# Expert weights by rank: no expert loaded twice, five buffers, and a last norm on token rows

## The chip, the cores and the metric

One core of a Trainium2 chip runs the whole program. The metric is the device time in microseconds (us) of one execution, the median of several.

## What is computed

One inference step of a two-layer backbone over 384 tokens of width 1024: 128 prompt tokens and 256 sample tokens, all float32. Each layer has a mixer (layer 0: mLSTM and MLA attention; layer 1: SSD and gated DeltaNet) and then a mixture of 32 SwiGLU experts, of which each token uses two. At the end comes an RMS norm over each token's 1024 channels. The change touches the experts and the last norm, so this is the part of the reference that matters:

```python
def rms_norm(x, g):
    y = xf * lax.rsqrt(jnp.mean(xf * xf, axis=-1, keepdims=True) + EPS)
    return (y * g.astype(jnp.float32)).astype(x.dtype)

def hier_moe(h, P, l):          # top-1 group of 4, then top-2 of its 8 experts
    glog = (x @ P['moe_w_group'][l] + P['moe_b_group'][l]).astype(f32)
    gsel = jnp.argmax(glog, axis=-1)
    elog = jnp.take_along_axis(elog, gsel[:, None, None], axis=1)[:, 0]
    tv, ti = lax.top_k(elog, MOE_TOPK)
    tw = jax.nn.softmax(tv, axis=-1) * gw
    eid = gsel[:, None] * MOE_PER_GROUP + ti
    hg = jnp.einsum('nd,edf->nef', x, P['moe_w_gate'][l])     # 1024 -> 256
    hu = jnp.einsum('nd,edf->nef', x, P['moe_w_up'][l])
    act = jax.nn.silu(hg) * hu * combine[..., None].astype(x.dtype)
    y = jnp.einsum('nef,efd->nd', act, P['moe_w_down'][l])    # 256 -> 1024

y_prompt = rms_norm(x, norm_final)      # and the same for y_sample
```

One expert's three matrices are 1 MiB each, 3 MiB together.

## The kernel before, in words

Five engines run their own instruction lists and wait for each other by semaphores. x, h and the mixer's output lie transposed in SBUF (channels on the 128 partitions, 8 blocks of 384 tokens): `xT`, `hT`, `mix`. Jobs of TensorE take the eight PSUM banks in rotation, in an order written out in `plan_jobs` (L160).

**Routing.** After the output projection (L870, L1100) TensorE turns the amplified rows back to tokens (`rows_out`, L1147) and ScalarE copies them, scaled, into `hrows`, which lies in `mix`; GpSimd adds the shift (L736) and SP writes them to memory (`h_rows_out`, L579). Meanwhile VectorE works out the router (L1991 to L2105): the two experts of each token, each token's rank inside its expert (by matmuls, `ranks`, L1123), and from these a slot. Expert e has 64 slots (`CAP`). One unit of work is a pair of blocks of 64 slots: pair q holds experts q and 16 + q. A 17th pair holds two spare blocks: an expert with 65 to 128 tokens gets one of them for those beyond 64, and is then loaded a second time (L2055 to L2064 choose, L2092 to L2101 give its number and the flag). If a third expert has more than 64, or one more than 128, the flag is set and all experts are computed densely instead (`dense`). `slot_lists` (L1137) turns the slots by matmuls into token numbers per slot (`slot_token`, L2086).

**A pair.** GpSimd gathers the pair's 128 rows by an indirect DMA (L745), TensorE transposes them (`turn`, L1170), ScalarE copies them to SBUF (L1607). Gate-up (L1183) is 32 matmuls of 512 columns, two at a time on the two halves of the array, one half for each block; silu (L1615) and the product (L2113) follow, a transposition (L1194), a copy (L2117), and the down product (L1208). ScalarE and VectorE scale the two halves of the rows (L1623, L2122), and GpSimd scatters them into `y_rows` in memory (L756). The turn of the next pair goes between gate-up and the transposition. After the last scatter SP reads the rows of each token's two experts back (L657), VectorE adds them (L2176), TensorE transposes them (L1264), and VectorE adds them to xT (L1984).

**Weights.** SP issues them (`load_pair`, L588): two buffers of a pair, one in the arena, one in the ring that the projections' weights use otherwise, so four experts in all. The first pair's go out before the output projection, the second's after it. The gate and up matrices of pair n (n from 2) wait for the gate-up of pair n - 2, its down matrices for the down product of pair n - 2. The order of the pairs is `ORDER`: the spare pair comes ninth, its two expert numbers are read from SBUF into SP's registers.

**The last norm.** ScalarE squares xT block by block (L1454), TensorE adds over the channels with a matrix of ones (L913), ScalarE takes the root (L1456), VectorE the reciprocal (L1781) and scales eight blocks by it and by the gain (L1788), TensorE turns them to token rows (L1426), ScalarE copies them to `mix` (L1742), and GpSimd issues the three output DMAs (L821).

## Time and profile before

| what | value |
|---|---|
| median of three runs (lowest, highest) | 1618.92 us (1618.03, 1621.61) |
| the profiled execution's own time | 1612.7 us |
| its span, first to last instruction | 1610.9 us |
| busy: TensorE, VectorE, ScalarE, GpSimd | 1317.4, 530.8, 343.9, 129.4 us |
| mean granted TensorE clock | 0.886 of full speed |
| moved by DMA | 341.77 MB, mean 212 GB/s |

A page line of a group has the form: line, engine, operation, output<-inputs and shapes, xcount, then busy us, mean ns of one, and the idle time of the engine ahead of it with what ended most of it. Line numbers are those of the kernel before. Times of the timeline and the chain are us from the span's start. A row "issue" is time for which the profile shows no releaser; SPq is SP's DMA issue.

### The profile page before, as it was taken

Reading aid. Unit: us, or ns where it says so; the run is one execution under the profiler, and the core shown is the slowest. Engines: PE = TensorE matmul, PEld = TensorE weight load, DVE = VectorE, ACT = ScalarE, POOL = GpSimd, SP = SyncE. Lnnn points to the kernel's source line nnn. Section 1 sums busy time; section 2 is a strip of 40 time slices with the busy share of each in tenths; the row PEclk is TensorE's granted clock in tenths of the full one; section 3 lists DMA queues with packets and bytes.
Section 4 is the critical chain, followed back from the end, with each engine's and each line's share of the span. In section 5 each row is a group of like instructions: output and inputs, shape, how many; then the busy total and the mean of one; then the engine's idle time right before and its main releaser. Section 6 shows DMA issues by size and latency. Waiting matters only on the chain.

```text
span 1610.9 us, 16071 instructions
## 1 busy us (share of the span) xinstructions
PE 1317.4 (82%) x6198; PEld 804.4 (50%) x6198; DVE 530.8 (33%) x1067; ACT 343.9 (21%) x720; POOL 129.4 (8%) x145
## 2 busy tenths in 40 slices
PE   5999799877986888878499997888859788888763
PEld 3545584344783333323266547787859633333322
DVE  3010652322233110101456907677651511010113
ACT  2100313322221111111326213222231211111102
POOL 2400100000011111110000001000000111111100
PEclk8999888877897999989799999999878789999986
DMA  9943565165534999997514100000034569999951
GB/s 340 322 152 106 189 192 209 55 224 191 184 124 180 420 423 422 420 413 290 204 57 153 66 13 1 27 1 1 1 105 183 196 255 422 423 421 419 405 206 72
DMA packets 82881, 341.77 MB, mean 212 GB/s; under 512 B 18967, under 2 KB 20161, under 8 KB 56560
## 3 DMA queue, kind: packets, MB, share of 16 engines
q1 hardware_dynamic: 67952, 313.09, 49.3%
q0 software_dynamic: 14848, 27.58, 5.3%
q8 instruction: 53, 0.87, 0.2%
q14 instruction: 28, 0.23, 0.0%
HBM read 333.11 MB, written 30.58 MB: 226 GB/s over the span
## 4 chain that ended last, share of the span: by engine, by line
PE 70%; DVE 14%; issue 9%; DMA 2%; ACT 2%; SPq 0%; POOL 0%; DVEq 0%; ACTq 0%; POOLq 0%
PE psum L870 19%; PE psum L1183 17%; PE psum L962 8%; PE psum L1208 8%; PE psum L894 3%; PE psum L1170 2%; PE psum L957 2%; DVE arena L2231 1%; DVE mix L2191 1%; PE psum L1083 1%; PE psum L1063 1%; PE psum L901 1%; DMA arena<-y_rows 1%; PE psum L913 1%; PE psum L1194 1%
## 5 line engine op out<-in xcount | busy, mean ns | idle before, releaser
L1183 PE MATMUL psum<-arena 128*64 128x512 f32 x576 | 153.1, 692 | 45.9 <-issue 43.6
L870 PE MATMUL psum<-hT,ring 128*128 128x384 f32 x448 | 152.4, 504 | 7.0 <-ACT hT L1463 5.1
L1183 PE MATMUL psum<-ring,arena 128*64 128x512 f32 x512 | 119.8, 622 | 19.4 <-issue 19.4
L962 PE MATMUL psum<-ring 128*128 128x128 f32 x872 | 114.8, 290 | 17.7 <-issue 8.4
L1183 PEld LDWEIGHTS psum<-arena 128*64 128x64 f32 x576 | 51.4, 158 | 146.4 <-issue 143.2
L2113 DVE TENSOR_TENSOR arena<-arena,psum 128x256 f32<-128x256 f32 x34 | 14.3, 421 | 332.9 <-ACT arena L1615 332.9
L870 PEld LDWEIGHTS psum<-hT,ring 128*128 128x128 f32 x448 | 88.3, 198 | 69.7 <-issue 12.8
L962 PEld LDWEIGHTS psum<-ring 128*128 128x128 f32 x872 | 109.1, 203 | 22.9 <-issue 13.1
L870 PE MATMUL psum<-ring,hT 128*128 128x512 f32 (+2 forms) x336 | 116.1, 507 | 0.0
L870 PE MATMUL psum<-mix,ring 128*128 128x384 f32 x256 | 91.7, 515 | 0.0
L1615 ACT ACTIVATE arena<-psum 128x256 f32<-128x256 f32 x34 | 13.1, 384 | 365.1 <-PE psum L1183 365.1
L1183 PEld LDWEIGHTS psum<-ring,arena 128*64 128x64 f32 x512 | 42.9, 143 | 95.6 <-issue 95.6
L870 PEld LDWEIGHTS psum<-ring,hT 128*128 128x128 f32 x336 | 58.3, 190 | 57.2 <-issue 56.4
L870 PEld LDWEIGHTS psum<-mix,ring 128*128 128x128 f32 x256 | 79.5, 316 | 5.8 <-issue 3.8
L1208 PE MATMUL psum<-arena 128*64 128x512 f32 x288 | 65.8, 598 | 9.3 <-DVE arena L2117 9.3
L756 POOL DMA_INDIRECT y_rows<-arena,slot_row x34 | 34.1, 1003 | 459.9 <-DVE arena L2122 430.3
L2122 DVE TENSOR_SCALAR arena<-psum,share 128x512 f32<-128x512 f32 x34 | 25.5, 751 | 127.8 <-PE psum L1208 127.8
L1208 PE MATMUL psum<-ring,arena 128*64 128x512 f32 x256 | 58.5, 599 | 8.3 <-DVE arena L2117 8.3
L894 PE MATMUL psum<-ring,sil 128*32 128x512 f32 x384 | 58.7, 762 | 6.2 <-issue 6.2
L736 POOL TENSOR_TENSOR mix<-mix,arena 128x1024 f32<-128x1024 f32 x6 | 14.1, 2369 | 509.1 <-ACT mix L1597 509.1
L1984 DVE SCALAR_TENSOR_TENSOR xT<-psum,modT,xT 128x128 f32<-128x128 f32 x64 | 23.8, 413 | 82.2 <-PE psum L870 79.6
L2231 DVE SCALAR_TENSOR_TENSOR arena<-arena,colsT 128x388 f32<-128x388 f32 x80 | 49.8, 623 | 2.8
(474 smaller groups left out, 1654.0 us busy)
## 6 DMA issues: line engine op xcount, KB each, us to landing
ring<-in_ada_w SPq DMA_DIRECT2D x24, 2048.0 KB, 10.6
arena<-in_moe_w_gate SPq DMA_DIRECT2D x36, 1024.0 KB, 11.9
arena<-in_moe_w_up SPq DMA_DIRECT2D x36, 1024.0 KB, 14.4
arena<-in_moe_w_down SPq DMA_DIRECT2D x36, 1024.0 KB, 17.5
ring<-in_moe_w_gate SPq DMA_DIRECT2D x32, 1024.0 KB, 14.1
ring<-in_moe_w_up SPq DMA_DIRECT2D x32, 1024.0 KB, 16.6
ring<-in_moe_w_down SPq DMA_DIRECT2D x32, 1024.0 KB, 18.2
ring<-in_w_in_odd SPq DMA_DIRECT2D x7, 2048.0 KB, 7.9
```

The costliest lines, as they stand in the source:

```text
L756: pool.indirect_dma_start(out=y_dram[l], out_offset=bass.IndirectOffsetOnAxis(ap=slot_row[:, q:q + 1].bitcast(U32), axis=0), in_=yrow[u], ...
L870: ins = mm(out, lhs(k), rhs(k), start=(k == 0), stop=(k == n - 1))
L894: ins = mm(b[at_:at_ + 32, :], sil[:, 4 * half + k, :], w[half][:, k, parity::2], start=(k == 0), stop=(k == 3), tile_position=(0, at_))
L901: ins = mm(b[:, 4 * m:4 * m + 4], mod_rows[:, m::4], pick, start=True, stop=True)
L957: ins = mm(b[:, tok(h)], col(h).to_broadcast([P, P]), ident, start=True, stop=True)
L962: ins = mm(b[:, h * width:(h + 1) * width], lhs(h), rhs(h), start=True, stop=True)
L1170: ins = nc.tensor.transpose(psum[:, k // 4, tok(k % 4)], hrow[q % 2][:, tok(k)], ident)
L1183: ins = mm(psum[half, 2 + s, :].rearrange("p (w f) -> p w f", w=2), hg[s][:, k, half], pair_gu[s][h][:, :, k, :], start=(k == 0), stop=(k ...
L1208: ins = mm(psum[half, 5 + n, :], act_s[s][:, j, half], pair_dn[s][h][:, j, 512 * n:512 * n + 512], start=(j == 0), stop=(j == 1), tile_pos ...
L1984: ins = stt(xT[:, m, t0:t1], bank(name, l, m)[:, t0:t1], modT[:, l, part, m, j:j + 1], xT[:, m, t0:t1], ALU.mult, ALU.add)
L2122: ts(yrow[q % 2][:, 512:D], psum[:, 6, :], share[:, ORDER[q]:ORDER[q] + 1], None, ALU.mult).then_inc(S(f"{kind}yb"), 1)
L2231: ins = stt(conv[:, i, :], cin[:, i, w:w + COUT], wcol[w], conv[:, i, :], ALU.mult, ALU.add)
```

## The change

**Units instead of pairs.** There are still 17 units. The first two hold experts 0 and 16, 1 and 17, as before. The next two are each a whole unit of 128 slots for one expert: the two experts with the most tokens (of all but 0, 16, 1, 17, 15, 31). The other units hold two experts of 64 slots. The places that the two fullest leave empty are filled by experts 15 and 31, whose own places were given up. So every expert is loaded once, 32 loads instead of 34, and from unit 2 on SP reads each expert's number from SBUF (`expert_id`, new) into a register. The flag is set if any expert has more tokens than slots.

**Five buffers.** Place n (one expert) goes to buffer n mod 5: two in the arena, two in the ring, and a new one over `hT` and `mix`, which now lie side by side as `wide`. Its load waits for the expert numbers and for the token rows' write to memory. Each place's gate and up matrices wait for the gate-up of the unit that used the buffer five places earlier, and its down matrix for that unit's down product; a unit's two gate-up loads stand ahead of its two down loads in SP's queue. The dense path computes its h anew from xT.

**The last norm** works on token rows: TensorE turns xT half by half (four blocks each) as soon as the residual adds allow, ScalarE squares the rows out of PSUM with a running sum, takes a root per tile, and VectorE scales out of PSUM into `mix` by the token's factor and the gain row, which GpSimd loads ahead of the second expert layer.

```diff
-SPARE = 2
-BLOCKS = EXPERTS + SPARE
-PAIRS = BLOCKS // 2
 HALF = EXPERTS // 2
-ORDER = list(range(HALF // 2)) + [PAIRS - 1] + list(range(HALF // 2, HALF))
-SPARE_AT = ORDER.index(PAIRS - 1)
+DOUBLES = 2
+AHEAD = 2
+BUFFERS = 5
+UNITS = [(2 * n, 2 * n + 1) for n in range(AHEAD)] + [(2 * AHEAD + n,) * 2 for n in range(DOUBLES)]
+UNITS += [(n, n + 1) for n in range(2 * AHEAD + DOUBLES, EXPERTS, 2)]
+PAIRS = len(UNITS)
+UNIT_OF = [next(u for u, two in enumerate(UNITS) if n in two) for n in range(EXPERTS)]
+MOVED = (HALF - 1, EXPERTS - 1)
+SINGLE = [h * HALF + n for n in range(AHEAD) for h in range(2)] + list(MOVED)
...
-    jobs += norm(4) + [("fin", c, k // 4) for c in range(TILES) for k in range(0, KD, 4)]
+    jobs += [("fin", c, half) for half in range(2) for c in range(TILES)]
...
+        def landed(l, n):
+
+            k = n % BUFFERS
+            return (EXPERTS + BUFFERS - 1 - k) // BUFFERS * l + n // BUFFERS + 1
...
-        hT = sb("hT", [P, KD, T])
-        mix = sb("mix", [P, KD, T])
+        wide = sb("wide", [P, 2 * KD * T])
+        hT = wide[:, 0:KD * T].rearrange("p (k t) -> p k t", k=KD)
+        mix = wide[:, KD * T:2 * KD * T].rearrange("p (k t) -> p k t", k=KD)
...
+        def expert_buffer(words):
+            return (words[:, 0:gate_up_words].rearrange("p (w k f) -> p w k f", w=2, k=KD),
+                    words[:, gate_up_words:gate_up_words + down_words].rearrange("p (j d) -> p j d", j=2))
+
+        one = gate_up_words + down_words
+        buffers = [(gu[n], dn[n]) for n in range(2)] + [expert_buffer(ring_words[:, n * one:(n + 1) * one]) for n in range(2)]
+        buffers += [expert_buffer(wide[:])]
...
-            def load_pair(l, n):
...
+            def load_unit(l, u):
+
+                kind = "gathered_"
+                weights_ = expert_weights(l)
+                which = sorted(set(UNITS[u]))
+                ids = []
+                for n in which:
+                    if u < AHEAD:
+                        ids.append(HALF * (n % 2) + u)
+                        continue
+                    at = n - 2 * AHEAD if u < AHEAD + DOUBLES else DOUBLES + HALF * (n % 2) + u - DOUBLES
+                    ids.append(sp.value_load(expert_id[0:1, l, at:at + 1], min_val=0, max_val=EXPERTS - 1))
+                for n, e in zip(which, ids):
+                    if n >= BUFFERS:
+                        sp.wait_ge(S(f"{kind}gu_computed"), PAIRS * l + UNIT_OF[n - BUFFERS] + 1)
+                    for w in range(2):
+                        sp.dma_start(buffers[n % BUFFERS][0][:, w],
+                                     weights_[w][bass.ds(e, 1)].rearrange("e (p k) f -> p (e k) f", k=KD))\
+                          .then_inc(S(f"{kind}gu{n % BUFFERS}_in"), 16)
+                for n, e in zip(which, ids):
+                    if n >= BUFFERS:
+                        sp.wait_ge(S(f"{kind}y1_computed"), PAIRS * l + UNIT_OF[n - BUFFERS] + 1)
+                    sp.dma_start(buffers[n % BUFFERS][1], weights_[2][bass.ds(e, 1)].rearrange("e (p j) d -> p (e j) d", j=2))\
+                      .then_inc(S(f"{kind}dn{n % BUFFERS}_in"), 16)
...
-                load_pair(l, 0)
+                load_unit(l, 0)
                 sp.wait_ge(*computed("o", l, KD - 1))
-                load_pair(l, 1)
+                load_unit(l, 1)
                 h_rows_out(l)
-                for n in range(2, PAIRS):
-                    load_pair(l, n)
+                sp.wait_ge(S("expert_ids"), l + 1)
+                sp.wait_ge(S("h_rows_out"), 16 * TILES * (l + 1))
+                for u in range(AHEAD, PAIRS):
+                    load_unit(l, u)
...
+                pool.wait_ge(S("odd_rows"), 2)
+                pool.dma_start(gain_row[:, 0:D], along(a["norm_final"])).then_inc(S("final_gain_in"), 16)
...
-                    pe.wait_ge(S(f"{kind}gu{s}_in"), 64 * loads(l, q))
+                    for n in sorted(set(UNITS[q])):
+                        pe.wait_ge(S(f"{kind}gu{n % BUFFERS}_in"), 32 * landed(l, n))
...
-            pe.wait_ge(S("h_final"), KD)
-            for c in range(TILES):
-                for half in range(2):
+            for half in range(2):
+                pe.wait_ge(*x_ready(4, 4 * half + 3))
+                for c in range(TILES):
                     b = issue("fin", c, half)
                     for k in range(4):
-                        ins = nc.tensor.transpose(b[:, tok(k)], hT[:, 4 * half + k, tok(c)], ident)
+                        ins = nc.tensor.transpose(b[:, tok(k)], xT[:, 4 * half + k, tok(c)], ident)
...
+            fn(rs_col[:, TILES:TILES + 1], eps[:, 0:1], ACT.Sqrt)
+            for half in range(2):
+                for c in range(TILES):
                     act.wait_ge(*computed("fin", c, half))
-                    dst = mix[:].rearrange("p k t -> p (k t)")[:, c * D:(c + 1) * D]\
-                        .rearrange("p (q k) -> p k q", k=KD)[:, 4 * half:4 * half + 4, :]
-                    fn(dst, heads(bank("fin", c, half), 4), ACT.Copy).then_inc(S("y_rows"), 1)
+                    done(fn(final_squares, bank("fin", c, half), ACT.Square,
+                            accum_out=row_sums[:, half, c:c + 1]), "final_sums")
+                    if half:
+                        fn(rs_col[:, c:c + 1], row_sums[:, 1, c:c + 1], ACT.Sqrt, scale=1.0 / D,
+                           bias=row_sums[:, 2, c:c + 1]).then_inc(S("final_roots"), 1)
+                if half == 0:
+                    done(fn(row_sums[:, 2, :], row_sums[:, 0, :], ACT.Identity, scale=1.0 / D, bias=eps[:, 0:1]), "final_sums")
...
-                o_(tt(prod, both, base_slot.unsqueeze(1).unsqueeze(1).to_broadcast(all4), ALU.mult))
-                o_(v.tensor_reduce(base_, prod, AX, ALU.add))
...
+                o_(stt(key, counts, 64.0, place, ALU.mult, ALU.add))
+                o_(v.tensor_reduce(top, key, AX, ALU.max))
+                o_(ts(doubled[:, 0, :], key, top, None, ALU.is_equal))
+                o_(stt(key2, doubled[:, 0, :], -1e7, key, ALU.mult, ALU.add))
+                o_(v.tensor_reduce(second, key2, AX, ALU.max))
+                o_(ts(doubled[:, 1, :], key2, second, None, ALU.is_equal))
+                o_(tt(shifts, doubled[:], delta, ALU.mult))
+                tt(room_, doubled[:, 0, :], doubled[:, 1, :], ALU.add)
+                tt(at_home, home, shifts[:, 0, :], ALU.add)
+                o_(v.tensor_reduce(hole_sum, shifts, AX, ALU.add))
+                ts(room_, room_, float(CAP), CAP + 0.5, ALU.mult, ALU.add)
+                o_(tt(at_home, at_home, shifts[:, 1, :], ALU.add))
+                o_(tt(at_home[:, HALF - 1::HALF], hole, hole_sum, ALU.subtract))
                 dve.wait_ge(*computed("rk", l))
                 order = bank("rk", l)[:, 0:TILES * EXPERTS].rearrange("p (c e) -> p c e", c=TILES)
                 where = R[11][:, :, 0:EXPERTS]
-                o_(stt(where, order, CAP + 0.5, bc(move, 1, [P, TILES, EXPERTS]), ALU.is_gt, ALU.mult))
-                take(tt(where, where, order, ALU.add), "rk", l)
+                tt(over, order, bc(room_, 1, [P, TILES, EXPERTS]), ALU.is_gt)
+                take(tt(where, order, bc(at_home, 1, [P, TILES, EXPERTS]), ALU.add), "rk", l)
+                o_(stt(where, over, float(OOB), where, ALU.mult, ALU.add))
                 o_(tt(prod, both, bc(where, 1, all4), ALU.mult))
                 o_(v.tensor_reduce(slot, prod, AX, ALU.add))
-                o_(tt(slot, slot, base_, ALU.add))
...
+                ids = R[3][0:1, 0, 0:DOUBLES + EXPERTS]
+                o_(tt(shifts[0:1], doubled[0:1], fill[0:1], ALU.mult))
+                tt(ids[:, DOUBLES:], iota[0:1, 0:EXPERTS], shifts[0:1, 0, :], ALU.add)
+                o_(v.tensor_reduce(fill_sum[0:1], shifts[0:1], AX, ALU.add))
+                tt(ids[:, 0:DOUBLES], vacant[0:1], fill_sum[0:1], ALU.subtract)
+                o_(tt(ids[:, DOUBLES:], ids[:, DOUBLES:], shifts[0:1, 1, :], ALU.add))
+                done(ts(expert_id[0:1, l, :], ids, 1.0, None, ALU.mult), "expert_ids")
...
+                take(tt(key, counts, room_, ALU.is_gt), "ct", l)
+                o_(v.tensor_reduce(too_many, key, AX, ALU.max))
+                done(ts(flag[0:1, l:l + 1], too_many[0:1], 0.5, None, ALU.is_gt), "flag")
...
+            dve.wait_ge(S("final_gain_in"), 16)
+            for c in range(TILES):
+                dve.wait_ge(S("final_roots"), c + 1)
+                o_(v.reciprocal(rs_col[:, c:c + 1], rs_col[:, c:c + 1]))
+                for half in range(2):
+                    part = slice(4 * half, 4 * half + 4)
+                    dst = mix[:].rearrange("p k t -> p (k t)")[:, c * D:(c + 1) * D]\
+                        .rearrange("p (q k) -> p k q", k=KD)[:, part, :]
+                    stt(dst, heads(bank("fin", c, half), 4), rs_col[:, c:c + 1], final_gain[:, part, :],
+                        ALU.mult, ALU.mult).then_inc(S("y_rows"), 1)
```

## Rows read from the trace of the kernel before

**Rows 1.** Page, part 2 (40 slices) and one line group of part 5.

```profile
DMA  9943565165534999997514100000034569999951
GB/s 340 322 152 106 189 192 209 55 224 191 184 124 180 420 423 422 420 413 290 204 57 153 66 13 1 27 1 1 1 105 183 196 255 422 423 421 419 405 206 72
...
L870 PE MATMUL psum<-hT,ring 128*128 128x384 f32 x448 | 152.4, 504 | 7.0 <-ACT hT L1463 5.1
```

**Rows 2.** Busy us by engine (x instructions), granted clock, DMA share and GB/s, two windows.

```profile
520.00:540.00 20.00, 19.18 (x96) 7.43 (x92) 2.29 (x5) 3.17 (x5) 4.05 (x4) 1.00 1.02 421
620.00:640.00 20.00, 16.01 (x66) 5.67 (x62) 1.60 (x3) 2.59 (x4) 2.01 (x2) 0.83 1.01 421
```

**Rows 3.** SP's weight issues in the first expert layer: start, us, first of each kind.

```profile
512.90 0.33 SPq L601 DMA_DIRECT2D arena<-in_moe_w_gate  x1
...
525.81 0.33 SPq L601 DMA_DIRECT2D ring<-in_moe_w_gate  x1
...
538.29 0.33 SPq L601 DMA_DIRECT2D arena<-in_moe_w_gate  x1
...
589.06 0.80 SPq L606 DMA_DIRECT2D ring<-in_moe_w_down  x2
601.46 0.37 SPq L601 DMA_DIRECT2D arena<-in_moe_w_gate  x1
```

**Rows 4.** TensorE's waits in the first and the second expert layer: us, times, longest.

```profile
PE psum L1183 <- issue: 30.1, 13, 4.0
...
PE psum L1183 <- issue: 32.9, 12, 4.7
```

**Rows 5.** The chain in the first expert layer, start and us.

```profile
543.87 6.87 PE psum L1183 x32
...
556.35 3.99 issue
560.34 9.82 PE psum L1183 x32
...
754.10 7.10 PE psum L1183 x32
```

**Rows 6.** First gather's issue; then gathers and scatters of two windows, us to landing.

```profile
497.18 1.08 POOL L745 DMA_INDIRECT arena<-h_rows,slot_token  x1 [12.72 <-DVE slot_token L2086]
...
arena<-h_rows,slot_token POOLq DMA_INDIRECT x1, 3.3
...
y_rows<-arena,slot_row POOLq DMA_INDIRECT x1, 8.2
arena<-h_rows,slot_token POOLq DMA_INDIRECT x1, 10.0
```

**Rows 7.** VectorE in the slot arithmetic: first and eleventh instruction, and after the lists.

```profile
487.28 0.19 DVE L2055 SCALAR_TENSOR_TENSOR crowded<-psum,cst 128x32 f32<-128x32 f32 x1
...
489.73 0.26 DVE L2068 SCALAR_TENSOR_TENSOR route<-psum,route 128x96 f32<-128x96 f32 x1 [0.20 <-PE psum L1133]
...
496.16 0.18 DVE L2086 TENSOR_SCALAR slot_token<-psum 128x17 int32<-128x17 f32 x1 [1.98 <-PE psum L1143]
```

**Rows 8.** The end of the kernel (timeline), and VectorE's row scaling (groups of instructions).

```profile
1577.32 6.19 DVE L1984 SCALAR_TENSOR_TENSOR xT<-psum,modT,xT 128x128 f32<-128x128 f32 x16 [1.07 <-PE psum L1264]
...
1585.96 0.58 ACT L1456 ACTIVATE rB<-psum,eps 128x384 f32<-128x384 f32 x1 [0.59 <-PE psum L913]
1586.64 2.55 DVE L1781 RECIPROCAL rB<-rB 128x384 f32<-128x384 f32 x1 [3.13 <-ACT rB L1456]
1589.23 4.32 DVE L1788 SCALAR_TENSOR_TENSOR hT<-xT,gains,rB 128x384 f32<-128x384 f32 x8
...
1593.61 4.33 PE L1426 MATMUL psum<-cst,hT 128*128 128x128 f32 x24 [7.69 <-DVE hT L1788]
1594.82 5.73 ACT L1742 ACTIVATE mix<-psum 128x512 f32<-128x512 f32 x6 [8.28 <-PE psum L1426]
...
L2122 DVE TENSOR_SCALAR arena<-psum,share 128x512 f32<-128x512 f32 x17 | 12.8, 751 | 63.9 <-PE psum L1208 63.9
```

125 lines of the change are left out of this document (45 added, 80 removed).

## The prediction

> **What bounds the kernel now.** I began with the page's slices [rows 1]. In two stretches, slices 13 to 18 and 33 to 37, the DMA digits stand at 9 and the rate at 405 to 423 GB/s; these are the expert layers. Elsewhere the rate is mostly below 260. Next came the busy times of two windows inside the first expert layer [rows 2]: the DMA share is 1.01 to 1.02 in both, at 421 GB/s, but TensorE is 96% busy in the first and 80% in the second, where its granted clock is 0.83, a mean between the two levels of 1.2 and 2.4 GHz. So the stage changes its bound. The chain shows where [rows 5]: the gate-up of a pair takes 6.87 us without a wait before it up to 543.87; the next one stands still for 3.99 us and then takes 9.82 us. TensorE's waits in each expert layer are put down to "issue" [rows 4], 13 times 30.1 us and 12 times 32.9 us. No engine released them, and only the weights' semaphores are left at that place, so these are landings. From the fifth pair on the weight stream is the bound, and TensorE is the bound for the first four pairs.
>
> Two prices follow. An unhindered pair costs TensorE what lies between the SP issues of two pairs, which wait for gate-ups: 525.81 - 512.90 = 12.9 us, then 538.29 - 525.81 = 12.5 us [rows 3]. A streamed pair costs more: gate-up 4 starts at 560.34, gate-up 16 at 754.10 [rows 5], 193.8 / 12 = 16.15 us, or 8.1 us per expert (3 MiB, with the gathers and scatters that run beside it). The stream itself starts at 512.90 [rows 3] and traffic some 1.6 us later. Up to gate-up 16 it carries 15 pairs less the last two down matrices, 29.33 experts: (753 - 514.5) / 29.33 = 8.13 us each. The two agree, so the stream never ran dry before, and a load that isn't made is worth its full 8.13 us as long as the stream stays the bound at the end.
>
> **The change, part by part, for one layer.** The sum is over the start of the last unit's gate-up; what comes behind it is the same.
>
> 1. Loads. 34 expert loads become 32. Units 0 and 1 are loaded early as before. Behind the restart there are then 28 experts instead of 30: 2 x 8.13 = 16.3 us less.
>
> 2. The fifth buffer. Expert place 4 goes into hT and mix, which are free once the token rows have been written to memory. Its load needs no gate-up of unit 0 any more, only the register value and that write. The expert numbers are worked out in the idle 1.98 us in which VectorE waits for the slot lists, ahead of the conversion at 496.16 [rows 7]; six instructions of at most 0.19 us fit there. So this load runs in a stretch in which the stream stands still, from about 498 to 506: another 8.1 us off the stream.
>
> 3. What is given back. TensorE now needs fewer experts for its first units (unit u needs 2u of them, where pair u needed 2u + 2), so it runs at 12.5 us per unit for longer, and the stream runs ahead until no buffer is free. By hand: the gate-up matrices of place 11 wait for unit 4's gate-up, which ends at 512.9 + 4 x 12.5 = 562.9, traffic from 564.5. The stream has by then carried places 5 to 10 without the last down matrix, 5.67 x 8.13 = 46.1 us, and is dry at 560.6: 3.9 us lost. From unit 9 on the stream is the bound again: TensorE could start it at 512.9 + 8 x 12.5 + 5.7 = 618.6, the stream has brought place 17's gate-up at 514.5 + 3.9 + 12.33 x 8.13 = 618.6.
>
> So far: last gate-up at 514.5 + 26.33 x 8.13 + 3.9 = 732.5 instead of 753, 20.5 us less.
>
> 4. The start is later. In the slot arithmetic the ten instructions from 487.28 to 489.73, 0.20 of it a wait for the ranks [rows 7], become thirteen, each (2.45 - 0.20) / 10 = 0.225 us, so 0.65 to 0.7 us more; two on the ranks become three; L2072 goes, and two more that ran under a wait. That is 0.7 + 0.3 - 0.2 less the wait of 0.20 that they now fill, 0.6, say 0.5 us. All of it is ahead of the first gather, hence of the first gate-up.
>
> 5. The first gather beside expert 4's load. Alone a gather lands in 3.3 us; it is issued at 497.18 [rows 6] and gate-up 0 hangs on it. Beside a full stream a scatter takes 8.2 us, and 10.0 for a gather queued behind one [rows 6]. So the new neighbour costs between 0 and 4.9 us. I take 2.8, because here the stream only begins as the gather does. The gathers of units 1 and 2 have the whole of gate-up 0 to land in.
>
> Steps 4 and 5 shift the restart of the stream 1:1: 3.3 us. A layer gains 20.5 - 3.3 = 17.2, with ends 20.5 and 20.5 - 0.5 - 6.7 (10.0 - 3.3) = 13.3. Two layers: 34.4, ends 26.6 and 41.
>
> A rule on step 5 is in the Trainium skill, "DMA: Bandwidth & Descriptors", section "Queues, rings and completion order": an engine alternates between the rings it has work for, a packet from each in turn, and so a gather does not queue behind all of expert 4's load. By it the wait grows with the gather's own packets only; if each waits for one like it, about 3.3 us more, and the two layers would give 33.4. The scatter's 8.2 beside a stream with no gap leans the same way as the rule, and neither excludes the other.
>
> 6. Costed at nothing. The new waits on SP (register values, rows written): queued behind them are all later loads, but the old queue stood there until 512.90 anyway. Reading the registers: the queue had two of these reads between the down issue at 589.06 and 601.46 [rows 3], where it waited for a gate-up in any case; the stream has more than a pair's work outstanding then, which is the cover. The gain row for the last norm (512 KB on POOL's queue) goes out before the expert layer, when the stream is idle. The flag is ready some us later, long before anyone asks for it. Matmuls per unit don't change in number or shape.
>
> **The last norm.** Residual adds end at 1577.32 + 6.19 = 1583.5 [rows 8]. Now come the sum over channels, the root 1585.96, a 384-wide reciprocal of 2.55, eight scalings of 4.32, transposes, and six copies that end at 1594.82 + 5.73 = 1600.55 [rows 8]. After: the transposes of half 0 go beside the residual adds, and so do their three squares. Behind the last add: four transposes (4/24 x 4.33 = 0.7, plus a 0.3 handover), one square with its sum on ScalarE (about 1.0, as one copy's 5.73/6), root and one-column reciprocal 0.5, then six scalings on VectorE. A 512-wide pass over PSUM takes 0.751 there [rows 8]; the new one writes with a stride, as the ScalarE copy did at 0.955. Six at 0.8 with two more reciprocals: 5.2. End 1583.5 + 1.0 + 0.2 + 1.0 + 0.5 + 5.2 = 1591.4, so 9.1 us less; with 1.13 per scaling 7. I take 9.
>
> **Sum.** 34.4 + 9 = 43.4 us off the profiled execution's 1612.7: 1569.3. That execution stands 6.2 us below the median of the three runs, 1618.92; the forecast is for the median, 1618.92 - 43.4 = 1575.5, written 1576.
>
> **The rivals.**
> A. Gather undisturbed. If the first gather lands before expert 4's descriptors matter, step 5 costs nothing: 1618.9 - 2 x 20 - 9 = 1570. For it: the first gather brings 21 rows in the first layer and 71 in the second, by the reference's choices. Against: they start within a microsecond of each other.
> B. Register reads hold up SP. No row times one by itself; the bound from above is half of 601.46 - 589.86, 5.8 us. Two now stand ahead of each unit's loads, between a down and the next gate-up load. As long as one takes under 2 us the outstanding work covers it; at 5.8 the stream would run dry early in each unit as long as TensorE sets the pace, and a layer loses a further 7 us: 1590. The Trainium skill, same page, "Latency and other measured facts", gives about 600 ns as the floor of such a read, by which this rival falls away.
> C. The early part brings nothing. The fifth buffer's 8.1 us is eaten by more starvation, as four buffers' worth of order is left and TensorE's pace is not kept (gate-ups of 9.82 instead of 6.87 in the first nine units too, as after the wait in rows 5). Then only the bytes count: 2 x (16.3 - 3.3) + 8 = 34 less, 1585.
> D. Slower: an expert that can't be doubled. The places of experts 0, 1, 15, 16, 17 and 31 are fixed, so one of these with over 64 tokens, which before got a spare block, now raises the flag, and all 32 experts are computed densely. A gate-up there would be 32 matmuls of 384 columns at 504 ns [rows 1], 16 us, so over 500 us a layer. It decides from one such expert on. Against it: counting the reference's choices on its inputs, over 64 are expert 28 in the first layer (71) and 22 and 23 in the second (67 and 70), none of the six.
> E. The change doesn't do what it says: if the double unit waited for a second landing the kernel would hang rather than be slow, so only a stream that isn't the bound is left. Rows 2 speak against it: then 1618.9 - 9 = 1610.
>
> **How the numbers follow.** Forecast's own case 0.5 (1567 to 1584), A 0.17, B 0.1, C 0.13, D 0.02, E 0.05, the rest is unnamed. The range 1562 to 1594 takes in A, B and C with the spread of the runs (3.6 us) at either end. About 0.2%, 3.2 us, is what can be told from no change. Faster by more 0.94, within 0.02, slower 0.04 (D and what I don't see).
>
> **What would show it.** In the profile after: places 4's load issued about 497, ahead of the first gate-up; turn 0 at 502 to 506 instead of 500.63; gate-ups 12.5 us apart up to unit 8 or 9, then waits of 2 to 4 us; TensorE's "issue" waits near 20 us per layer instead of 30; weights 12.6 MB fewer; last ScalarE copies gone, three roots in their place, end some 8 us behind the last residual add. Wrong would be: gate-ups 16 us apart from unit 4 on, a DMA rate that falls under 400 for more than 5 us after 520, or a first gate-up later than 512.

## The result, and the profile after

The changed kernel takes 1591.82 us, the median of four runs (1590.08 to 1592.47); beside it the kernel before took 1620.26 (four runs, 1618.03 to 1624.00). The ratio is 0.9828, with a 95% interval from 0.9808 to 0.9849. So 28.4 us went, where 43.4 were forecast. The direction is right and the time lies in the range, near its upper end; a third of the forecast gain is missing, and the runs below are about that third.

The page of the changed kernel, parts 2 and 5, beside [rows 1]:

```profile
PEclk9999888777695999899799999989787969999996
DMA  9942565055517799998514200000017259999943
GB/s 343 333 150 106 188 199 212 0 212 212 187 52 286 287 391 418 418 419 353 202 54 150 75 14 0 4 25 1 1 41 264 119 201 407 398 418 418 417 195 122
...
L1204 PE MATMUL psum<-cst,arena 128*128 128x128 f32 x272 | 38.8, 288 | 18.9 <-DMA arena<-h_rows,slot_token 18.9
```

The first expert layer shows 9 in four slices of the DMA line instead of five, the second in five as before, and their middle runs at 417 to 419 GB/s instead of 419 to 423. The last row is new: turn 0 waited 18.9 us in the two layers for the first gathers.

The timeline of the changed kernel from the first gather to the second unit (start, us, engine, line; in brackets the idle time before and what ended it), beside [rows 3, 6]:

```profile
504.78 0.37 SPq L630 DMA_DIRECT2D wide<-in_moe_w_gate  x1
...
505.72 0.38 SPq L636 DMA_DIRECT2D wide<-in_moe_w_down  x1
527.55 0.35 SPq L630 DMA_DIRECT2D arena<-in_moe_w_gate  x1
...
532.65 0.33 SPq L636 DMA_DIRECT2D arena<-in_moe_w_down  x1
534.31 0.33 SPq L630 DMA_DIRECT2D arena<-in_moe_w_gate  x1
...
505.88 1.09 POOL L777 DMA_INDIRECT arena<-h_rows,slot_token  x1 [12.85 <-DVE slot_token L2130]
...
514.19 1.94 PE L1204 MATMUL psum<-cst,arena 128*128 128x128 f32 x8 [9.42 <-DMA arena<-h_rows,slot_token]
517.30 9.62 PE L1218 MATMUL psum<-arena 128*64 128x512 f32 x32 [1.17 <-ACT arena L1642]
```

Place 4's load goes out 1.1 us ahead of the gather. The gather lands 8.2 us after its issue, where it took 3.3 alone. From 532.65 to 534.31 SP issues a down load, reads two registers and goes on: 1.33 us behind the issue, 0.67 for a read and what goes with it.

The chain of the same layer, beside [rows 5], and TensorE's waits from 500 to 770, beside [rows 4]:

```profile
595.02 6.89 PE psum L1218 x32
602.07 0.33 SPq L630
602.50 18.23 DMA arena<-in_moe_w_up
620.98 7.10 PE psum L1218 x32
...
726.76 24.16 DMA arena<-in_moe_w_up
750.93 0.28 issue
751.20 7.10 PE psum L1218 x32
```

```profile
PE psum L1204 <- DMA arena<-h_rows,slot_token: 9.4, 1, 9.4
PE psum L1218 <- DMA arena<-in_moe_w_up: 8.8, 4, 3.9
...
PE psum L1218 <- DMA ring<-in_moe_w_up: 6.3, 3, 3.9
PE psum L1218 <- DMA wide<-in_moe_w_up: 5.4, 2, 3.5
```

Gate-ups are 12.5 us apart up to unit 7; unit 8's, at 620.98, is the first to wait, and from there a unit takes 16.3 us ((751.20 - 620.98) / 8). The waits for weights add to 8.8 + 6.3 + 5.4 = 20.5 us, where "issue" stood with 30.1; in the second layer they add to 24.1, where it stood with 32.9.

The end (timeline), beside [rows 8]:

```profile
1565.03 6.19 DVE L2018 SCALAR_TENSOR_TENSOR xT<-psum,modT,xT 128x128 f32<-128x128 f32 x16 [1.08 <-PE psum L1300]
...
1572.02 0.60 ACT L1775 ACTIVATE arena<-psum 128x512 f32<-128x512 f32 x1 [0.71 <-PE psum L1461]
...
1573.37 2.17 DVE L2424 SCALAR_TENSOR_TENSOR wide<-psum,rs_col,gain_row 128x512 f32<-128x512 f32 x2
...
1577.90 2.17 DVE L2424 SCALAR_TENSOR_TENSOR wide<-psum,rs_col,gain_row 128x512 f32<-128x512 f32 x2
```

The last scaling ends at 1580.07, 8.85 us behind the last residual add (1571.22); before, the last copy ended 17.04 us behind it.

**One layer measured in two parts.** The document goes on with three landmarks. T0 and T16 are the ends of the first and the last gate-up (the start of ScalarE's activation behind them). Between them lies the fall-off, the first of two slices of 1 us in a row in which the DMA engines move under 380 GB/s, at the end of the layer's stream. "Full" is from T0 to the fall-off, "tail" from there to T16. The tail ends with the last gate-up itself, so the table also has that gate-up's own time and the stretch from T0 to its start, which is what the forecast was over: 20.5 us shorter. Where the text says stream, it means T0 to T16. Per layer, mean of both layers, in us:

```
kernel                       full    tail   T0 to T16   last gate-up   T0 to its start   first gather (layer 0, 1)
before, two profiles        235.4    13.5     248.8         7.5            241.3         3.3, 3.9 / 3.3, 3.7
after, two profiles         215.5    17.4     232.9         8.2            224.7         8.2, 8.3 / 8.1, 8.4
held gather                 215.3    18.9     234.3         9.4            224.8         3.3, 4.0
place 4 loaded late         220.8    19.5     240.3         8.5            231.8         3.4, 4.1
before, spare not loaded    225.2    12.3     237.5         7.1            230.4         3.4, 4.0
second double at 14         212.7    18.7     231.4         7.9            223.4         3.4, 4.1
doubles at 8 and 14         212.3    19.8     232.1         7.1            225.0         3.3, 4.3
held gather, no scatters    213.4     9.9     223.3         8.0            215.3         3.4, 4.1
rows spread                 216.5    14.0     230.4         7.9            222.6         3.1, 3.9
rows in stride 8            214.4    19.7     234.1         7.1            227.0         3.2, 4.3
rows spread, double at 14   213.3    14.7     228.0         7.1            220.8         3.0, 3.8
```

The full part became 20.0 us shorter, the tail 3.9 us longer, and the last gate-up starts 16.6 us earlier. The boundary between full and tail is good to a slice, about 1 us. Single layers differ: the tail was 13.2, 11.8, 13.8 and 15.0 us before and 15.3, 18.8, 15.6 and 20.0 after. Part of that is TensorE's clock in the last gate-up, which took between 7.1 and 10.1 us. First the kernel after (the gate-up at 751.20), then the kernel with the held gather (744.27), whose TensorE had waited 3.17 us ahead of it:

```profile
751.20:758.30 7.10, 7.09 (x32) 2.62 (x32) 0.36 (x1) 0.00 (x0) 0.99 (x1) 1.00 0.14 53
```

```profile
744.20:754.30 10.10, 10.01 (x32) 3.13 (x32) 0.00 (x0) 0.00 (x0) 0.00 (x0) 0.70 0.10 38
```

The granted clock was 1.00 in the one and 0.70, a mean between the two levels, in the other.

**The same stretch in bytes.** From T0 to the start of the last gate-up the DMA engines moved 99.3 MB before and 90.2 MB after: 9.1 MB less, 21.7 us at 420 GB/s. Against that rate they lost 4.8 us before and 9.9 after, 5.1 more: 2.5 in the idle stretch of step 3, 1.5 in the first 25 us behind T0, 0.8 behind the fall-off, the rest spread. 21.7 - 5.1 = 16.6. By the fall-off alone they had moved 10.1 MB less, so 1.0 MB more is left for the tail, 2.4 us of its length.

The fall-off in slices of 1 us; the first row is of the kernel before, from 730 to 770, the second of the kernel after, from 710 to 750:

```profile
GB/s 442 426 418 401 410 410 442 426 426 418 442 397 463 402 410 426 410 442 328 270 229 197 188 188 123 115 217 57 20 4 0 0 0 0 0 0 0 0 8 66
```

```profile
GB/s 410 410 426 426 418 426 418 410 426 434 410 418 426 377 442 406 410 418 414 418 418 426 426 410 426 410 426 426 410 430 430 418 385 360 328 311 279 303 262 205
```

### The profile page after: what moved, and what is told of

It reads as the page before. It is cut to its first block, busy times and chain, and to the rows that moved or that the text cites. A ratio compares the mean times of both kernels' runs of the same rounds, so it can differ in the third digit from the quotient of the medians.

```text
span 1590.6 us, 16451 instructions
## 1 busy us (share of the span) xinstructions
PE 1306.8 (82%) x6182; PEld 798.6 (50%) x6182; DVE 528.8 (33%) x1064; ACT 338.9 (21%) x722; POOL 130.4 (8%) x146
## 4 chain that ended last, share of the span: by engine, by line
PE 59%; DMA 18%; DVE 13%; issue 6%; ACT 2%; SPq 1%; POOL 0%; DVEq 0%; ACTq 0%; POOLq 0%
PE psum L904 20%; PE psum L1218 11%; PE psum L996 9%; DMA ring<-in_moe_w_up 6%; DMA arena<-in_moe_w_up 5%; PE psum L1244 3%; PE psum L928 3%; DMA wide<-in_moe_w_up 3%; PE psum L991 2%; DVE arena L2269 1%; DVE wide L2229 1%; PE psum L1097 1%; PE psum L1117 1%; PE psum L935 1%; DMA arena<-h_rows,slot_token 1%
## 5 line engine op out<-in xcount | busy, mean ns | idle before, releaser
L904 PE MATMUL psum<-wide,ring 128*128 128x384 f32 x704 | 242.9, 506 | 7.0 <-ACT wide L1498 5.1
L904 PEld LDWEIGHTS psum<-wide,ring 128*128 128x128 f32 x704 | 167.4, 240 | 74.7 <-issue 15.4
L1218 PE MATMUL psum<-arena 128*64 128x512 f32 x480 | 160.6, 667 | 24.5 <-DMA ring<-in_moe_w_up 11.8
L1218 PE MATMUL psum<-ring,arena 128*64 128x512 f32 x384 | 133.1, 611 | 12.1 <-DMA wide<-in_moe_w_up 10.8
L904 PE MATMUL psum<-ring,wide 128*128 128x512 f32 (+2 forms) x336 | 116.1, 507 | 0.0
L1218 PE MATMUL psum<-wide,arena 128*64 128x512 f32 x224 | 90.8, 623 | 10.3 <-DMA arena<-in_moe_w_up 10.3
L904 PEld LDWEIGHTS psum<-ring,wide 128*128 128x128 f32 x336 | 58.3, 190 | 57.2 <-issue 56.4
L1244 PE MATMUL psum<-arena 128*64 128x512 f32 x240 | 73.0, 598 | 8.3 <-DVE arena L2153 8.3
L1244 PE MATMUL psum<-ring,arena 128*64 128x512 f32 x192 | 65.7, 598 | 6.2 <-DVE arena L2153 6.2
L1204 PE MATMUL psum<-cst,arena 128*128 128x128 f32 x272 | 38.8, 288 | 18.9 <-DMA arena<-h_rows,slot_token 18.9
L1204 PEld LDWEIGHTS psum<-cst,arena 128*128 128x128 f32 x272 | 30.5, 145 | 45.2 <-issue 45.2
## 6 DMA issues: line engine op xcount, KB each, us to landing
arena<-in_moe_w_up SPq DMA_DIRECT2D x28, 1024.0 KB, 22.6
ring<-in_moe_w_up SPq DMA_DIRECT2D x24, 1024.0 KB, 18.9
```

What stands on the lines that cost most here:

```text
L904: ins = mm(out, lhs(k), rhs(k), start=(k == 0), stop=(k == n - 1))
L1204: ins = nc.tensor.transpose(psum[:, k // 4, tok(k % 4)], hrow[q % 2][:, tok(k)], ident)
L1218: ins = mm(psum[half, 2 + s, :].rearrange("p (w f) -> p w f", w=2), hg[s][:, k, half], buffers[UNITS[q][h] % BUFFERS][0][:, :, k, :], star ...
L1244: ins = mm(psum[half, 5 + n, :], act_s[s][:, j, half], buffers[UNITS[q][h] % BUFFERS][1][:, j, 512 * n:512 * n + 512], start=(j == 0), sto ...
```

## The experiments

Twelve runs, on three chips, each set beside runs of the kernel before on the same chip: 1619.73 in the first set, 1620.73 in the second, 1619.62 in the third.

**1. The kernel after, a second time.** No edit.

> The changed kernel itself, as the standard for the others of this set, and a second profile of it. Theory clock: the 8 us by which the first expert layer began later in the profile of after than in that of before (weights of unit 1 issued at 478.6 instead of 470.0) lie in code that the change did not touch and come from where the granted clock fell in the attention stage, so this start moves by several us from one profile to the next; here anywhere from 466 to 482. Rival layout: the change did it (other SBUF addresses, a larger table), then 478 to 479 again. Time 28 us below before.

1586.97 us (1585.56 to 1592.27), ratio 0.9797 (0.9776 to 0.9818), so 32.8 us less. The second profile gives streams of 231.6 and 235.2 us, the first 231.4 and 233.4, and the first gathers agree to 0.1 us. But layer 0 begins elsewhere: unit 1's weights are issued at 475.3, against 478.3 in the first profile and 470.0 in that of the kernel before. That speaks against the rival, which wanted 478 to 479 again.

**2. The last norm alone.** The kernel before with the norm on token rows, experts untouched:

```
+            for half in range(2):
+                pe.wait_ge(*x_ready(4, 4 * half + 3))
+                for c in range(TILES):
+                    b = issue("fin", c, half)
                     for k in range(4):
-                        ins = nc.tensor.transpose(b[:, tok(k)], hT[:, 4 * half + k, tok(c)], ident)
+                        ins = nc.tensor.transpose(b[:, tok(k)], xT[:, 4 * half + k, tok(c)], ident)
...
```

> Only the last norm is changed, the experts are those of before. By the rows of the two profiles the stretch from the start of the last residual adds to the last write of the output rows went from 23.2 to 15.0 us, so 8.2 us below before, ratio 0.995. If the adds themselves or the output transfers took the gain back, the ratio is over 0.997. Rival layout for the start of the first expert layer: it is at 470 as in before; theory clock: anywhere from 462 to 482.

1612.07 us (1602.29 to 1616.15), ratio 0.9942 (0.9918 to 0.9966): 7.7 us. In its trace the last scaling again ends 8.9 us behind the last add. The norm is worth about 8 us (5.5 to 13.3 by the interval). Its experts are those of before, and yet unit 1's weights go out at 475.3, as in the second profile of the kernel after.

**3. The gather held free of the load.** In the kernel after, SP waits for the first gather before it issues place 4's load:

```
                 for u in range(AHEAD, PAIRS):
+                    if u == AHEAD:
+                        sp.wait_ge(S("gathered_hrow0_in"), 16 * loads(l, 0))
                     load_unit(l, u)
```

> After, but SP waits with the load of place 4 until the first gather has landed. Theory: the first gather took 8.2 and 8.3 us instead of 3.3 and 4 because this load runs beside it; held back, the gather lands in 3.3 to 4 us, the load still ends before the first gate-up does, and each layer ends 4.5 us earlier: 9 us below after. Rival: the gather is slow for another reason (its place in the queue, the memory it reads), then it takes 8 us again and the later load costs nothing or a little: 0 to 4 us above after.

1580.61 us (1570.89 to 1585.96), ratio 0.9750 (0.9720 to 0.9779), 6.4 us faster than the kernel after on the same chip, where 9 were expected; the two intervals just touch. From its chain:

```profile
504.48 3.27 DMA arena<-h_rows,slot_token
...
507.88 1.96 PE psum L1205 x8
```

The gather is back at 3.3 and 4.0 us. So the neighbour had cost 4.9 and 4.4 us, about the 4.9 that step 5 named as the most it could cost. The load, now issued at 508.80, still lands just before the stream restarts (519.82, T0 519.94), and the last gate-up starts as far behind T0 as in the kernel after, 224.8 against 224.7 us. The 1.4 us per layer that the stream is longer are the last gate-up's: it took 9.4 us on average instead of 8.2, by the clock. By its median this kernel beats both.

**4. Place 4 loaded late.** The fifth buffer is there, but its load waits for unit 0's gate-up:

```
                 for u in range(AHEAD, PAIRS):
+                    if u == AHEAD:
+                        sp.wait_ge(S("gathered_gu_computed"), PAIRS * l + 1)
                     load_unit(l, u)
```

> After, but the load of place 4 waits for the first gate-up, as the first load behind the restart did in before: the fifth buffer's head start is gone, the saved loads stay. Theory (the prediction's terms, corrected to what after shows): 4.6 us per layer back from the gather, 7.5 us of weights added to the stream, 2 us less starvation, so 1 us per layer above after, 0 to 4 us in all. If the head start is worth its full 8.1 us per layer: 7 us above after. If it was worth nothing: 9 us below after, as hold_gather.

1591.15 us (1587.66 to 1596.87), ratio 0.9823 (0.9798 to 0.9849), 10.5 us slower than the held gather and 4.2 slower than the kernel after, whose interval it overlaps. The last gate-up starts 231.8 us behind T0, against 224.8 held and 224.7 after: loading place 4 ahead is worth 7.0 us a layer, the idle stretch that comes with it already taken off. This kernel doesn't have that stretch. In the kernel after it is where step 3 put it, from 572 on, 46 us behind T0 (rate in slices of 1 us, from 560 to 600):

```profile
GB/s 418 434 410 430 402 430 414 434 422 402 410 410 393 352 287 307 180 160 176 438 430 418 410 442 434 418 410 369 397 422 418 430 401 438 418 418 401 418 451 434
```

The seven slices from 393 to 176 miss 2.6 us of full rate, and the same stretch of the second layer 1.7; 3.9 were forecast.

**5. The price of a load.** The kernel before, without the spare pair's loads; the two spare experts are computed with what lies in the buffers:

```
             def load_pair(l, n):
...
+                if n == SPARE_AT:
+                    return
...
-                    pe.wait_ge(S(f"{kind}gu{s}_in"), 64 * loads(l, q))
+                    if q != SPARE_AT:
+                        pe.wait_ge(S(f"{kind}gu{s}_in"), 64 * weights_in(l, q))
```

> The kernel before, without the weight loads of the spare pair (12.6 MB fewer in the two layers); TensorE does not wait for them and multiplies what lies in the buffers, so the two spare experts come out wrong and the times stay comparable. Theory of the prediction: two loads are worth 16.3 us of the stream between the first and the last gate-up, the stream falls from 248.5 to 232, and the kernel becomes 32 us faster. Rival (the price was read with the gathers' and scatters' bytes in it, and these remain, 7.5 us of a load is its own): the stream falls by at most 15.0, to 233.5. Second rival (the buffers, not the bytes, set part of it: four buffers cannot hold what the freed 15 us of the queue could bring, a sum over the waits of the queue gives 9.5): 239, and 19 us in all.

1598.17 us (1596.41 to 1598.79), ratio 0.9860 (0.9838 to 0.9882), 22.6 us less; the stream is 237.5, 11.3 shorter. The second rival (239, and 19 us in all) is nearest. Windows of this kernel (us, busy us and count by engine, clock, DMA share, GB/s):

```profile
580.00:600.00 20.00, 15.27 (x66) 6.00 (x68) 2.35 (x4) 2.10 (x3) 4.04 (x4) 0.93 1.01 421
600.00:620.00 20.00, 17.56 (x84) 6.91 (x80) 1.60 (x3) 2.10 (x3) 2.02 (x2) 0.98 0.72 297
620.00:640.00 20.00, 18.97 (x96) 7.53 (x96) 3.19 (x6) 4.19 (x6) 2.03 (x3) 1.00 0.94 379
```

Here the queue stands still for 20 x (0.29 + 0.07) = 7.2 us in the first layer and 6.0 in the second. The full part is 10.2 shorter; with the idle 6.6 that makes 16.8 for two loads, 8.4 each. That looks like the 8.13 of the prediction, but the boundary of the full part moved: by the fall-off 6.8 MB less had passed, while the loads left out are 6.3 MB, 15.0 us at 420 GB/s. From T0 to the start of the last gate-up it is 6.5 MB, 7.75 us a load, between a load's own 7.5 and 8.13. What a removed load brings depends on the buffers that are there to use its time.

**6 and 7. The doubled units elsewhere.** The held gather, with the second doubled unit at place 14, or both at 8 and 14. The slot constants and the register indices follow the list; with both moved, place 4's down matrix is also issued ahead of place 5's loads, so that the fifth buffer is filled as before:

```
+DOUBLE_AT = (2, 14)
+PAIR_AT = [u for u in range(PAIRS) if u not in DOUBLE_AT]
...
-        hole = 2 * CAP * (AHEAD + n) - 1
+        hole = 2 * CAP * DOUBLE_AT[n] - 1
```

> The kernel after with the held gather, and the second of the two doubled units moved from place 3 to place 14 in the order; the same bytes, the same buffers, the same router instructions. Theory (two units with one load each in a row, where TensorE takes 12.5 us a unit and a load 7.5, leave the DMA engines idle for lack of a free buffer, and near the end nothing covers the last pair): the stream of each layer becomes 3 to 5.5 us shorter than with the held gather (234.3), 6 to 11 us in all, a time of 1570 to 1575. Rival (the stream is set by the bytes behind the first gate-up and by the slowest DMA engine's lag at its end): 234, no change against the held gather.

1576.40 us (1573.68 to 1578.27), ratio 0.9728 (0.9706 to 0.9751). The stream is 231.4, 2.9 us a layer shorter than with the held gather and just short of the 3 to 5.5 expected; 1.5 of that is again the last gate-up's own time, and its start is 1.4 earlier. The idle stretch is gone; first the held gather, then this kernel:

```profile
560.00:580.00 20.00, 19.48 (x96) 6.98 (x92) 2.35 (x4) 2.79 (x4) 4.05 (x4) 1.00 0.91 361
```

```profile
560.00:580.00 20.00, 19.48 (x94) 6.84 (x90) 2.35 (x4) 2.10 (x3) 4.04 (x4) 1.00 1.01 419
```

So what two doubled units in a row give back is a real term, and it can be had: by the fall-off the DMA engines had lost 3.3 us instead of 6.3. Of that, 1.3 us go again in the tail, where the loss up to the last gate-up is 5.2 us instead of 3.9. On the whole time it isn't shown, as the two intervals overlap.

> As the one before, with both doubled units moved, to places 8 and 14, so that the first seven units ask for two loads each. Theory of idle DMA engines: as much gained as with one moved, or up to 1 us a layer more (by a sum over the waits of the queue 4.5 to 5.5 us shorter than 234.3), and the slices behind the first gate-up show the DMA engines full. If the idle stretches come from the queue's order (a down load that waits holds up the next expert's loads), they stay, and it is 2 to 4 us a layer slower than with one moved.

1579.28 us (1573.19 to 1584.92), ratio 0.9755 (0.9731 to 0.9779), a stream of 232.1: no better, within what these runs can tell, than with one moved. The full part is 0.3 shorter, the tail 1.1 longer.

**8. Without scatters.** The held gather, each indirect scatter replaced by a write of one row, so that the experts' outputs don't reach the tokens:

```
-                        pool.indirect_dma_start(out=y_dram[l], ..., in_=yrow[u], ...)
+                        pool.dma_start(y_dram[l][n:n + 1, :], yrow[u][0:1, :])
```

> The kernel after with the held gather, and in place of each indirect scatter a write of one row (4 KB), so that the tokens' experts are not summed into the output; 3.1 MB fewer in each layer. Theory (a load's measured 8.13 us held gathers and scatters): the stream shortens by the scatters' bytes in its DMA-bound part, 10 of 17 units, 4.5 us a layer, up to 7.5 if all of it is DMA-bound, so 9 to 15 us in all against the held gather. Rival (the scatters go beside the loads at no cost, and a load is worth 8.13 by itself): no change, 234.

Its own time, 2612.03 us (ratio 1.6116, 1.6083 to 1.6150), says something else: with the first layer's experts missing, the second layer's router overfilled its places and the kernel went through its dense path, 1031 us more than the held gather takes. That is the price of rival D, forecast as over 500. The streams ahead of it can be read: 224.1 and 222.5, so 11.0 us a layer less; up to the start of the last gate-up it is 9.5, still more than both theories gave. The full part lost only 1.9, in part because the idle stretch grew: the loss by the fall-off is 7.7 us instead of 6.3. The tail fell from 18.9 to 9.9, and only 1.9 of that is not the last gate-up itself (8.0). Most of the scatters' cost is in the tail.

**9 and 10. The same rows, elsewhere in a unit.** An expert's tokens take its first rows, some 24 of 64 on average; the rest is skipped. A constant decides which partition a row is:

```
-    c[:, C_IOTA:C_IOTA + P] = np.arange(P)
+    r = np.arange(CAP)
+    for h in range(2):
+        c[:, C_IOTA + CAP * h + (11 * r + 8 * h) % CAP] = CAP * h + r
...
```

and, for the other, `(8 * (r % 8) + r // 8)` in place of `(11 * r + 8 * h) % CAP`. Bytes and instructions stay the same.

> The kernel after with the held gather, and a changed constant: the n-th token of an expert no longer takes the n-th of its 64 rows but row (11 n) mod 64, the second expert's shifted by 8. Same bytes, same instructions. A unit's real rows (24 of 64 on average, the others are skipped) then lie all over the partitions instead of at the start of each half. Theory (the scattered and gathered rows fall on a part of the 16 DMA engines, which lag in the weight stream, and its end waits for them): the 16 parts of a transfer land closer together, by 1000 to 2000 ns instead of 7 us apart in the last 60 us, the last gate-up's wait behind the fall-off of the stream goes from 8 us to about 4, the stream from 234.3 to 227 to 231, 7 to 14 us in all against the held gather. Rival (rows are dealt to the engines evenly wherever they lie; the lag is that of the software queue as such): 234, no change.

> The same with another order: the n-th token takes row 8 (n mod 8) + n / 8, so the tokens are even over the blocks of eight partitions, but 16 neighbouring tokens fall on rows that are 0 or 1 mod 8. If a block of eight partitions goes to one engine, this is as good as the other order (227 to 231 a layer). If partition p goes to engine p mod 16, it is worse than the held gather (over 236). If neither matters, 234.

Spread: 1574.46 us (1568.75 to 1579.97), ratio 0.9722 (0.9694 to 0.9750); stream 230.4, tail 14.0. Stride 8: 1580.66 us (1578.25 to 1587.52), ratio 0.9770 (0.9746 to 0.9794); stream 234.1, tail 19.7. The full parts differ from the held gather's by 1 us, the tails of the two from each other by 5.7, and the last gate-up starts 222.6 and 227.0 us behind T0, against 224.8. So where the rows lie decides 4.5 us a layer, and it decides them in the tail. The whole times say the same, 6.2 us apart, with intervals that just touch; that the spread beats the held gather they don't show. Each load lands in sixteen parts, each with its own record. I had expected them 1 to 2 us apart with the spread; they landed up to 10.5 and 12.3 us apart in the two layers, against 13.8 and 14.8 held. For the second kernel neither of my two maps of partitions to DMA engines gave the right answer, but its rates say which one would. In the first layer, from 730 to 770, and in the second, from 1497 to 1537 (slices of 1 us):

```profile
GB/s 279 213 225 213 213 213 213 221 205 213 221 205 213 213 156 140 82 57 8 0 0 0 0 0 0 0 0 0 8 140 70 0 111 311 430 406 426 410 410 434
```

```profile
GB/s 422 410 410 451 418 418 410 434 434 410 402 303 250 213 213 213 205 213 213 221 156 123 107 106 98 99 90 0 0 0 0 0 0 0 0 0 0 25 82 37
```

In the first layer the rate stands at 213 for 13 us, half of 426: eight of sixteen engines had work left, all about the same. In the second it stands at 213 for 7 us and then near 105, a quarter: four engines. The Trainium skill, "DMA: Bandwidth & Descriptors", section "The descriptor swizzle", gives a map under which this comes out: a transfer over 128 partitions goes to each engine as four neighbouring partitions and the four that lie 32 further on, engines 0 to 7 for the lower half of the partitions and 8 to 15 for the upper. The page states it for a plain transfer of the software queue; the plateaus of this run agree with it for gathers and scatters. By that map and the reference's choices the engines carry these numbers of token rows in a layer, each row once gathered and once scattered:

```
                      layer 0, engines 0-7 / 8-15                     layer 1
as the kernel after   88 77 66 57 47 34 28 28 / 66 59 55 45 44 31 27 16    88 88 75 59 48 41 39 32 / 76 62 51 35 23 20 17 14
spread                80 48 44 70 38 54 59 32 / 49 27 62 42 34 54 36 39    85 51 48 79 44 60 63 40 / 39 18 66 29 31 53 20 42
stride 8              94 20 91 18 86 16 85 15 / 90  1 86  1 84  1 79  1    94 30 91 29 88 28 83 27 / 73 10 68  9 64  7 60  7
```

Stride 8 loads eight engines alike in the first layer, and in the second four of them most, as seen. It would also say why the spread gained only 2.3 of the 9.5 us that the scatters cost: its fullest engine still carries 80 and 85 rows where 48 would be even. As an estimate, a row is 8 KB through its engine, 0.31 us at a sixteenth of 420 GB/s: against the 88 rows of the kernel after the spread should gain 2.5 and 0.9 us in the two layers (2.7 and 1.8 measured against the held gather) and stride 8 lose 1.9 in both (4.0 and 0.5), so the map explains the order and not the exact sizes. A constant made for this map, row r at partition 4 (r mod 8) + r / 8 within each 32, would leave 60 and 66 rows on the fullest engine; it was not run.

**11. Rows spread and the double at 14.** Both edits.

> The row order of the first of these and the second doubled unit at place 14 together. If lag and idle stretches are separate terms, their gains add: 2.9 us a layer from the place, measured, and what the row order gives, so 224 to 229 a layer and 1560 to 1570 in all. If the late double had only hidden the lag of the last pair, it gives nothing on top of the row order.

1572.33 us (1570.53 to 1575.08), ratio 0.9713 (0.9689 to 0.9737): stream 228.0, the full part near that with the double alone (213.3), the tail near that of the spread alone (14.7). The two gains add: 1.4 and 2.3 against 4.0 up to the start of the last gate-up, 2.9 and 3.9 against 6.3 in the streams. The time is above the 1560 to 1570 expected. This is the fastest version by its median, 47.3 us below the kernel before, though its interval overlaps those of the spread alone, of the double alone and of the held gather.

**12. The kernel before, a second profile.** No edit.

> The kernel before, unchanged, for a second profile. Theory of the clock (the 8.3 us by which layer 0's experts began later in the profile after are no work of the change): the issue of unit 1's weights lies anywhere between 470 and 478 us, the stream is 248 to 250 in both layers. If that start is again at 470.0 within 0.5, the change did delay it, and the cause is to be sought in the new layout.

One time, 1620.65, with a span of 1618.9, 8 us longer than the first profile's 1610.9. Unit 1's weights go out at 474.8. One of the windows in which the profiles differ, in code that no edit touches; first the kernel before, then its second profile, then the kernel after:

```profile
280.00:320.00 40.00, 33.23 (x109) 12.83 (x107) 14.17 (x34) 13.61 (x25) 0.00 (x0) 0.91 0.10 34
```

```profile
280.00:320.00 40.00, 35.76 (x103) 12.90 (x102) 11.68 (x25) 12.14 (x19) 0.00 (x0) 0.79 0.01 2
```

```profile
280.00:320.00 40.00, 35.76 (x103) 12.88 (x102) 11.74 (x25) 12.15 (x19) 0.00 (x0) 0.79 0.01 2
```

The same program ran this stretch at a granted clock of 0.91 once and 0.79 once, between the two levels of 1.2 and 2.4 GHz, with TensorE busy 83% and 89% of the time. Over all profiles unit 1's weights go out between 470.0 and 475.3 with the experts of before (four profiles) and between 469.1 and 478.4 with those of after (ten). So the start moves by several us by itself, and nothing shows that the change delays it.

## Why the prediction was right in direction and 15 us too high in gain

Term by term, per layer, with two profiles of each kernel where there are two:

- **Steps 1 to 3, the stretch up to the start of the last gate-up: -20.5 forecast, -16.6 measured.** The mechanism is right, and two terms were mis-sized.
- **The price of a load, 8.13 us, was too high.** Three loads fewer were to bring 24.4 us. The bytes that passed fell by 21.7 us' worth at 420 GB/s. The 8.13 was the whole stretch divided by the experts, so it held the gathers' and scatters' bytes and the loss at the stream's end, and these don't go away with a load; a load's own bytes are 7.5 us. The full part alone, 20.0 us shorter, seems to confirm the 20.5, but that is luck: 2.4 of it is 1.0 MB that now passes behind the fall-off.
- **What is given back: 3.9 forecast, 5.1 measured.** The idle stretch of step 3 came at the place and time forecast, with 2.5 us. A further 1.5 lie in the first 25 us behind T0, where step 6 cost the queue's order at nothing: at 527.55 two loads go out, and the next in the queue is a down matrix that waits until 532.65, where the kernel before had put four loads out. In the kernel with its second double at 14 unit 3 has two experts, so four loads go out again, and the loss in these 25 us is 1.8 us, against 1.6 before and 3.1 after. The last 0.8 are behind the fall-off: the working took the last gate-up to start when its share of bytes had passed at the mean rate, but a gate-up waits for the slowest of sixteen parts. Experiment 8 shows that this end belongs mostly to the scatters, 9 and 10 that it is a matter of where their rows lie.
- **What comes behind the start of the last gate-up "is the same":** 7.5 us before, 8.2 after, by the clock of single profiles.
- **Step 4, the router: 0.5 forecast, not to be told from nothing.** From unit 1's weights to the first gather it is 27.16 and 27.14 us in the first profile before, but 27.39 and 27.82 in the second, and 27.63, 27.28, 27.36 and 27.35 after.
- **Step 5, the first gather: 2.8 forecast, 4.9 and 4.4 measured.** The right mechanism, mis-sized. The reason for the lower value, "because here the stream only begins as the gather does", was a hope against the row that it was nearest to, a scatter's 8.2 us beside a full stream [rows 6]. The 3.3 us that the prediction worked out with the Trainium skill's rule of packets in turn ("DMA: Bandwidth & Descriptors", section "Queues, rings and completion order") were too few as well. That the gather doesn't wait for the whole load the trace bears out: it landed at 514.1, behind place 4's gate and up matrices (509.6 and 512.8) and 1.9 us ahead of its down matrix (515.9).
- **Step 6, the register reads, held.** Two of them take 1.33 us between two issues, and rival B falls. The Trainium skill, "DMA: Bandwidth & Descriptors", section "Latency and other measured facts", gives about 600 ns as the floor of a `tensor_load`, the name of these reads in the trace; the trace agrees, the second starts 0.58 us after the first.
- **The last norm: 9 forecast, 7.7 measured alone, 8.2 in the trace.** The scaling takes 1.09 us (2.17 for two), not 0.8. Its write has a stride and it has a second operand from SBUF, and no run tells the two apart. The prediction's other end, 1.13, which gave 7, has no row behind it.

Summed: 2 x (16.6 - 0.7 - 0.1 - 4.7) + 8 = 30.2, beside a measured 28.4 and 32.8. Of the 13.2 us between this and the forecast 43.4 the terms of the stream make 7.8, the gather 3.8, the last gate-up's clock 1.4, the norm 1, and the router takes 0.8 off. The base was right: the profiled execution of before, 6 us below its median, was a quick one (experiment 12), and setting the gain against the median was needed.

Of the rivals, A falls with the gather's 8.2, C with the 12.5 us from unit 0 to unit 7 and the full part, E with both. D didn't occur on these inputs, and its price was twice the bound given. No rival named what happened: a load worth less than its price, more idle time, and a later end. In reading the page the prediction also took slice 18 to stand at 9; it stands at 7, with 290 GB/s, and nothing hangs on it.

Of the signs, place 4's load and turn 0 came where forecast once the 8.3 us of the later start are taken off (496.5, 505.9), the first wait at unit 8, none longer than 3.9 us (4.2 in the second layer), and 12.0 MB fewer on the page (the gain row adds 0.5). Two signs that were to mean "wrong" appeared without being so: a first gate-up behind 512 (517.30, of which 8.3 are the later start), and more than 5 us under 400 GB/s after 520, which is step 3's own gap. A sign must be measured from a landmark near it, and must not contradict the sum.

**Open.** Why the tail is longer with five buffers (17.4 to 19.8 where the rows lie as before) than with four (12.3 to 13.5). A part may be the halves in which the moved and the doubled experts now lie: by the same map and choices the fullest engine carries 84 and 83 rows before and 88 in both layers after, an estimated 1.2 and 1.6 us. For the rest the landing records fit one reading: the sixteen parts of a transfer landed up to 8.1 and 10.4 us apart near the end of the two layers before, 13.7 and 15.1 after, 16.5 and 16.8 with place 4 late, 6.4 and 7.1 without scatters. An engine with few rows can run ahead of the others as far as there are free buffers, and a fifth lets it go further. That is argued; no run changed the number of buffers alone.

## What to carry to other kernels

A stream of loads ended here when its slowest DMA engines did: beside indirect transfers, look at the rate in slices of 1 us at its end, and count which partitions the real rows of a gather or scatter lie in; the constant that spread them cost no instruction. Price a load that is to go by its own bytes, and not by the stream's length over the number of loads, which holds everything that stays. Where two stretches end with a piece of TensorE's work, compare them up to its start, so that the clock of one profile isn't read as a cost. A load that is removed from a bound queue is worth its full price only if buffers are free to use the time; where units with less to load stand in a row, the queue idles, so put them apart. And before a load is moved into an idle stretch, ask which small transfer the critical path is waiting for there: holding the load back until the gather had landed gave 6.4 us by the medians.
